# Two stacked transformer blocks on one core: the edges between ten stages done by halves of the tokens

## What is computed

```python
for l in range(2):                       # first block, 512 tokens
    f = swiglu(rmsnorm(x, g), w_gate, w_up, w_down)        # stage "F1"
    x = x + 0.5 * rmsnorm(f, post_g)
    m = token_mixing(rmsnorm(x, g), w_in, ..., w_out)      # stage "M1": three kinds of attention
    x = x + rmsnorm(m, post_g)
    f = swiglu(rmsnorm(x, g), ...)                         # stage "F1" again
    x = x + 0.5 * rmsnorm(f, post_g)
h = concatenate([meta_tokens, x])
for l in range(2):                       # second block, 528 tokens
    h = mixer_sublayer(h, ...)           # stage "M2": attention, convolutions, w_out, norm, residual
    h = ffn_sublayer(h, ...)             # stage "F2": as swiglu, with a 3-tap convolution on the hidden features
```

## Time and profile before

| | us |
|---|---|
| median of 3 runs | 3659.04 (3654.0 to 3659.16) |
| the profiled execution, its own time | 3653.45 |
| its span, first to last instruction | 3651.7 |
| PE busy | 3451.0 (95%) |
| PE weight loads busy | 2940.5 (81%) |
| DVE busy | 1738.8 (48%) |
| ACT busy | 1378.0 (38%) |
| POOL busy | 458.4 (13%) |
| mean granted TensorE clock | 0.968 of full |

### The profile page before, as it was taken

How to read it: one execution, slowest core, us unless ns; L and a number is a source line. 1 busy time by engine, 2 the same in 40 slices (tenths; PEclk the granted TensorE clock), 3 DMA queues, 4 the chain that set the end, 5 groups by cost and what they waited for, 6 DMA issues and landing times.

```text
span 3651.7 us, 54900 instructions
## 1 busy us (share of the span) xinstructions
PE 3451.0 (95%) x20422; PEld 2940.5 (81%) x20422; DVE 1738.8 (48%) x2244; ACT 1378.0 (38%) x2224; POOL 458.4 (13%) x253
## 2 busy tenths in 40 slices
PE   7999899899998999899899998988999999889998
PEld 5888666578886888666688887878999988789997
DVE  4442456444424442456444315734664266356642
ACT  3332345432224232345433323564443245534431
POOL 2000222200001000322200004202000132110000
PEclk9999999899999999899899998998999999989998
DMA  4333311123232332312133322212222221122232
GB/s 133 98 92 95 90 53 59 52 81 97 89 96 76 92 97 90 90 53 58 47 92 92 95 90 64 53 39 70 88 90 88 87 65 50 47 64 90 88 93 70
DMA packets 329965, 287.71 MB, mean 79 GB/s; under 512 B 9089, under 2 KB 325593, under 8 KB 329781
## 3 DMA queue, kind: packets, MB, share of 16 engines
q1 hardware_dynamic: 327344, 281.63, 26.0%
q10 hardware_dynamic: 2245, 3.50, 0.3%
q0 software_dynamic: 192, 0.14, 0.1%
HBM read 283.10 MB, written 5.27 MB: 79 GB/s over the span
## 4 chain that ended last, share of the span: by engine, by line
PE 87%; DVE 4%; issue 3%; ACT 3%; POOL 1%; ACTq 0%; DVEq 0%; DMA 0%; POOLq 0%
PE ps L546 24%; PE ps L547 24%; PE ps L548 24%; DVE x L676 2%; PE ps L1485 2%; PE ps L1487 1%; PE ps L1486 1%; PE ps L1070 1%; PE ps L1094 1%; PE ps L1107 1%; PE ps L578 1%; PE ps L588 1%; DVE S L670 1%; ACT xhi L616 1%; PE ps L1534 1%
## 5 line engine op out<-in xcount | busy, mean ns | idle before, releaser
L546 PE MATMUL ps<-xhi,whi 128*128 128x512 f32 (+1 forms) x3296 | 1140.6, 346 | 7.0 <-ACT r L608 5.2
L547 PE MATMUL ps<-xlo,whi 128*128 128x512 f32 (+1 forms) x3296 | 1132.4, 344 | 0.0
L548 PE MATMUL ps<-xhi,wlo 128*128 128x512 f32 (+1 forms) x3296 | 1128.8, 342 | 0.0
L529 DVE TENSOR_TENSOR wlo<-raw,whi 128x1024 fp32r<-128x1024 f32 (+1 forms) x426 | 510.8, 1199 | 1285.2 <-ACT whi L523 1282.2
L523 ACT ACTIVATE whi<-raw 128x1024 fp32r<-128x1024 f32 (+1 forms) x536 | 555.0, 1037 | 1303.4 <-PE ps L548 1243.3
L546 PEld LDWEIGHTS ps<-xhi,whi 128*128 128x128 f32 x3296 | 625.4, 190 | 99.3 <-issue 24.8
L548 PEld LDWEIGHTS ps<-xhi,wlo 128*128 128x128 f32 x3296 | 623.3, 189 | 74.6
L547 PEld LDWEIGHTS ps<-xlo,whi 128*128 128x128 f32 x3296 | 624.6, 189 | 71.8 <-issue 0.5
L548 PE MATMUL ps<-hhi,wlo 128*128 128x512 f32 (+1 forms) x1408 | 477.6, 339 | 0.0
L546 PE MATMUL ps<-hhi,whi 128*128 128x512 f32 (+1 forms) x1408 | 476.5, 338 | 0.0
L547 PE MATMUL ps<-hlo,whi 128*128 128x512 f32 (+1 forms) x1408 | 476.2, 338 | 0.0
(11 more groups left out here) (247 smaller groups left out, 3916.5 us busy)
## 6 DMA issues: line engine op xcount, KB each, us to landing
raw<-in_ffn_w_up_dram SPq DMA_DIRECT2D x176, 512.0 KB, 3.6
raw<-in_ffn_w_down_dram SPq DMA_DIRECT2D x120, 512.0 KB, 3.5
raw<-in_w_in_dram SPq DMA_DIRECT2D x94, 512.0 KB, 3.8
raw<-in_ffn_w_gate_dram SPq DMA_DIRECT2D x88, 512.0 KB, 3.8
raw<-in_w_out_dram SPq DMA_DIRECT2D x32, 512.0 KB, 3.5
raw<-in_ffn_w_down_dram SPq DMA_DIRECT2D x24, 256.0 KB, 2.8
tbias_scratch<-rev_scratch ACTq DMA_DIRECT2D x1, 3072.0 KB
y<-tbias_scratch SPq DMA_DIRECT2D x2, 1536.0 KB, 6.9
```

The costliest lines, as they stand in the source:

```text
L529: eng.tensor_tensor(wlo[slot][:, 0:n], raw[slot][:, 0:n], whi[slot][:, 0:n].bitcast(F32), ALU.subtract).then_inc(b.s.weights_split, 1)
L546: pe.matmul(o, wh, hi[:, t0:t0 + w], start=first, stop=False)
L547: pe.matmul(o, wh, lo[:, t0:t0 + w], start=False, stop=False)
L548: ins = pe.matmul(o, wl, hi[:, t0:t0 + w], start=False, stop=last)
```

## The change

Every edge is done in two halves of the tokens (256 and 256, or 264 and 264):

- Output tiles. In F stages the last pair of output chunks (m=3), in M stages the last two pairs (m=2 and 3), are made half by half (`pe_late`): first all remaining tiles for the tokens of half 0, then for half 1. Their weights must then be held all at once; they get homes in memory that is free by then (`home`: parts of the hidden tile, or of the attention's buffers).
- Norm. The squares are summed by a matmul against a full 128x128 tile of ones, in f32, which leaves the sum on all partitions (`pe_post_sum`, three matmuls; `pe_pre_sum`, one), and ACT makes the inverse root as exp(-0.5 ln(...)) for each half (`act_norm`). `pe_square_sum`, `act_rms`, `dve_inv`, `pe_spread`, `act_r` are gone.
- New x. `dve_edge` handles two chunks of one half in an instruction where it can (128 x 2 x 256): scaled y, new x, and xlo chunk by chunk. The post gain is applied when ACT copies y. The squares of new x go to y and are added by DVE (`dve_x_sum`), no longer by POOL.
- First granules. The next stage's first three granules (before: two) are split ahead, by ACT and DVE, into three `whi`/`wlo` buffers, and `pe_first` does them for half 0, then for half 1.
- The layer loops are written out, and waits outside the inner loops are on constants. The bias table of M1 is loaded later, in three DMAs. At the start x comes in two DMAs and the small loads of POOL move to SP behind them; at the end the output is stored as its quarters are ready.

The core of the diff:

```diff
+        def pe_post_sum(pe, g, h):
+            t0, w = OUT[g][h]
+            o = ps[:, sum_bank(g, "post 0") if h == 0 else sum_bank(g + 1, "post 1"), 0:w]
...
+            pe.matmul(o, ones[:, 0:P], acc[:, t0:t0 + w], start=True, stop=False)
+            pe.wait_ge(e.y_squared, 8 * (g + 1) - (1 - h) * len(LATE[g]))
+            pe.matmul(o, ones[:, 0:P], sq[0][:, t0:t0 + w], start=False, stop=False)
+            pe.matmul(o, ones[:, 0:P], sq[1][:, t0:t0 + w], start=False, stop=True).then_inc(e.norm_sums, 1)
...
+        def pe_first(pe, b, g, gb, tiles, rest=()):
...
+            for h, (t0, w) in enumerate(IN[g]):
+                pe.wait_ge(e.out_free, max(OUTS[g] - 1 + h, 0))
+                for p in range(4):
+                    now = [(n, t) for n in range(2) for t in tiles[n] if t[2] // 2 == p]
+                    pe.wait_ge(e.x_hi, 8 * g + 4 * h + p + 1)
+                    for n in range(2):
+                        if h == 0 and any(n == i and t is tiles[n][0] for i, t in now):
+                            pe.wait_ge(b.s.weights_split, gb + n + 1 + CR)
+                        for _, (bank, wcol, c, start, stop) in [i for i in now if i[0] == n]:
+                            for wt in (whi, wlo):
+                                pe.matmul(view(bank, h), wt[n][:, wcol:wcol + P], xhi[:, c, t0:t0 + w],
+                                          start=(start and wt is whi), stop=False)
+                    pe.wait_ge(e.x_lo, 8 * g + 4 * h + p + 1)
+                    for n, (bank, wcol, c, start, stop) in now:
+                        ins = pe.matmul(view(bank, h), whi[n][:, wcol:wcol + P], xlo[:, c, t0:t0 + w],
+                                        start=False, stop=stop)
+                        if h == 1 and (bank, wcol, c, start, stop) == tiles[n][-1]:
+                            ins.then_inc(b.s.granules_done, 1)
+                    if h == 0 and p == 1 and g > 0:
+                        pe_post_sum(pe, g - 1, 1)
+                if h == 0:
+                    pe.wait_ge(b.s.weights_split, gb + 2 + 1 + CR)
+                else:
+                    pe_pre_sum(pe, g, 0)
+                half = len(tiles[2]) // 2
+                for t in tiles[2][:half]:
+                    tile(h, 2, t)
+                if h == 1:
+                    pe_pre_sum(pe, g, 1)
+                for t in tiles[2][half:]:
+                    ins = tile(h, 2, t)
+            if rest:
+                pe.wait_ge(e.norm_log, pre(g, 1))
+                for t in rest:
+                    for h in range(2):
+                        ins = tile(h, 2, t)
...
+        def act_norm(act, idx, bank, dst):
+            w = dst.shape[1]
+            act.wait_ge(e.norm_sums, idx)
+            act.activation(dst, ps[:, bank, 0:w], ACT.Ln, bias=eps[:, :], scale=1.0 / D).then_inc(e.norm_log, 1)
+            act.wait_ge(e.norm_log, idx)
+            act.activation(dst, dst, ACT.Exp, scale=-0.5).then_inc(e.norm_made, 1)
...
+        def dve_edge(dve, g, ch, factor, nxt, third=None):
+            for h in range(2):
+                dve.wait_ge(e.norm_made, post(g, h))
...
+                scaled(0)
+                for p in range(4):
+                    x2 = x[:, 2 * p:2 * p + 2, c0:c0 + w]
+                    ch.wait()
+                    dve.tensor_tensor(x2, x2, t2(p), ALU.add).then_inc(e.x_new, 1)
+                    if p < 3:
+                        scaled(p + 1)
+                    if h == 0 and p == 1 and third is not None:
+                        third()
+                    if nxt is not None and p > 0:
+                        dve_x_lo(dve, g + 1, nxt, h, p - 1)
+                if nxt is not None:
+                    dve_x_lo(dve, g + 1, nxt, h, 3)
+                    dve_x_sum(dve, g + 1, h, ch)
...
+        def pe_late(pe, b, g, gb, qs, hi, lo):
...
+            for h in range(2):
+                n = 0
+                for m in LATE[g]:
...
+                    for q in range(whole, nq):
...
+                        for k in qs[q]:
+                            for o in range(2):
+                                ins = tile(h, m, q, k, o)
+                                n += 1
+                                if h == 1 and n == POST_AFTER:
+                                    pe_post_sum(pe, g, 0)
...
+            nxt = PRE[KIND_AT[g + 1]]
+            for p in range(3):
+                act_x_hi(act, g + 1, nxt, 0, p)
+            for p in range(2):
+                act_x_square(act, g + 1, 0, p)
+            act_ypart(act, b, g, gb, nq, 3, 1, col)
+            act_x_hi(act, g + 1, nxt, 0, 3)
+            act_post_norm(act, g, 1)
+            for p in (2, 3):
+                act_x_square(act, g + 1, 0, p)
+            for p in range(4):
+                act_x_hi(act, g + 1, nxt, 1, p)
+                act_x_square(act, g + 1, 1, p)
```

More of the change, by code:

```diff
@@ new lines, in act_pre_norm, with act_x_hi @@
+        def act_pre_norm(act, g, h):
+            t0, w = IN[g][h]
+            act_norm(act, pre(g, h), sum_bank(g, f"pre {h}"), r[:, t0:t0 + w])
+        def act_x_hi(act, g, col, h, p):
+            t0, w = IN[g][h]
+            c0, _ = xcols(g, h)
+            act.wait_ge(e.x_new, 8 * g + 4 * h + p + 1)
+            for c in (2 * p, 2 * p + 1):
+                ins = act.activation(xhi[:, c, t0:t0 + w], x[:, c, c0:c0 + w], ACT.Copy, scale=gain(col, LAYER[g], c))
+            ins.then_inc(e.x_hi, 1)
@@ L662, in act_yevac @@
             for o in range(2):
[L663 to L683 removed]
+                c = 2 * m + o
@@ L703, in pe_up_granule @@
                 pe.wait_ge(b.s.hidden_free, f.ev(l) + 2 * i + q // 2 + 1)
+            apart = isinstance(i, int) and not b.conv
             for o in range(2):
@@ L713, in pe_up_granule @@
-                if o == 0 and between is not None:
-                    between()
+                    bank, wcol = 4 * (q // 2) + 2 * o, kk * PAIR + o * P
+                    if apart:
+                        for h, (t0, w) in enumerate(IN[0]):
+                            ins = part_mm(pe, ps[:, bank + h, 0:w], whi[q % 2][:, wcol:wcol + P],
+                                          wlo[q % 2][:, wcol:wcol + P], xhi[:, k, t0:t0 + w], xlo[:, k, t0:t0 + w],
+                                          False, kk == 3)
+                        continue
@@ L715, in pe_up_granule, with pe_out @@
+                    ins = tile_mm(pe, b, bank, q % 2, wcol,
+                                  xhi[:, k, :], xlo[:, k, :], first and kk == 0, not first and kk == 3)
             ins.then_inc(b.s.granules_done, 1)
-        def pe_out(pe, b, l, sub, gb, qs, hi, lo, ready, second=None, order=None, begun=0):
+        def pe_out(pe, b, g, gb, qs, hi, lo, ready=None, second=None, begun=0):
             nq = len(qs)
-            def pair_of(base, m, mi):
-                pe.wait_ge(b.s.out_free, 4 * sub + base + m + 1)
+            for m in range(begun, LATE[g][0]):
+                if m == 1 and second is not None:
+                    second()
+                if m == 2:
+                    pe.wait_ge(e.out_free, OUTS[g] + 1)
@@ L774, in pe_ffn @@
+        def pe_ffn(pe, b, g, f):
+            l = LAYER[g]
+            tiles = [[(4 * (q // 2) + 2 * o, kk * PAIR + o * P, 4 * (q % 2) + kk, q % 2 + kk == 0, q == 1 and kk == 3)
+                      for kk in range(4) for o in range(2)] for q in range(3)]
+            rest = []
+            if b.conv:
+                tiles[2], rest = tiles[2][0::2], tiles[2][1::2]
+            pe_first(pe, b, g, f.gb(l), tiles, rest)
             pe_up_granule(pe, b, l, f, 0, 3)
```

874 lines of the change are left out of this document (467 added, 407 removed).

## The result

| | before | after |
|---|---|---|
| median, us | 3658.53 (4 runs) | 3537.32 (4 runs, 3533.23 to 3539.5) |
| ratio | 1 | 0.9669 (0.9657 to 0.9681) |
| span of the profiled execution, us | 3651.7 | 3534.8 |
| mean granted TensorE clock | 0.968 | 0.988 |

The kernel is 121 us faster; 159 were forecast. The spans differ by 116.9. I read first the same cuts as in the earlier trace rows: each from the end of half 0 of the late tiles to the first matmul behind the granules that are done by halves (three into M1, M2 and F2; four into F1). The first line is the start up to its second loop, the eighth the end; the three lines behind the mark are stretches between edges.

The account below looks back on a forecast made before the run. PE, 95% busy, was taken as the bound, with gains only at edges. Span 3651.7 - 144 (edges) - 13 (end) + 4 (start) - 6 (M stages) = 3492.7 us; median 3659.04 - 159 = 3500, range 3458 to 3560.

Parts of the forecast that it names:

- The edge: Nine transitions between stages: step-by-step timeline of F1 to M1; all nine to cost 76 us in place of 220, minus 144.
- The end: Kernel end, behind the last output tiles: 17 us instead of 30.3, minus 13, bounds 9 to 16.
- The start: Kernel start: later loads and four more table loads against half 0 starting early; plus 4 us, bounds -3 to +12.
- The small loads behind x: At the start: small loads queued behind 2 MB of x on SP, making DVE 0 to 7 us later.
- Inside the M stages: Four attention stages: written-out loops drop register arithmetic ahead of waits, 1.5 us a stage, minus 6, bounds 0 and 20.
- the weights cost nothing: At edges: seven granules load in about 22 us within 25; if cover fails, one or two us an edge.
- rival 2: Edges: clock falls to 1.2 GHz at new gaps, plus 8 us an edge, 3572; milder mixtures 3530 to 3570; 0.19 together.
- rival 1: Edges: half 1's waits are hidden by ACT and DVE overlap, 2 to 3 us an edge, 3445 to 3465; chance 0.14.
- rival 3: Narrow matmuls: held by weight loads of 0.190 us, 192 us more over 2628 matmuls, 3692; chance 0.03.
- The drain at a table load: Start: a skill page's 1.38 us drain per table switch, five loads 6.9 us more, start plus 11; chance 0.03.

Follow-up runs that it names:

- experiment 4: Changed kernel with squares and their sums in fp32r tiles, so the matmuls against ones run in reduced precision: 3514.69 us, ratio 0.9602.
- experiment 5: Changed kernel with one load of the table set holding both Ln and Exp ahead of the first stage: 3529.03 us, ratio 0.9643.
- experiment 6: Changed kernel with the third granule split by ACT and DVE behind half 0 of x at the start, instead of ahead: 3533.57 us, ratio 0.9654.
- experiment 2: Changed kernel with ACT's whole queue around the attention stages' late tiles reordered, third granule's low part made inside the edge: 3513.12 us, ratio 0.9602.
- experiment 1: Changed kernel with only ACT's evacuation of output pair m=1 in attention stages moved, between the sixth and seventh late granules' splits: 3541.15 us, ratio 0.9676.
- experiment 7: Changed kernel with ACT's wait for the table's store and its issue of the 3 MB copy moved behind its setup activations: 3536.76 us, ratio 0.9664.
- experiment 8: Changed kernel with three start edits: third granule behind half 0 of x, one table load, 3 MB copy behind ACT's setup: 3524.05 us, ratio 0.9628.
- experiment 10: Kernel with all winning edits and half 0's additions moved later, plus the 3 MB copy issued behind ACT's squares of first x: 3461.45 us, ratio 0.9455.

## Why the prediction was right, and where it was off

- **The edge.** The timeline that I drew up for F1 to M1 holds nearly step by step. With time 0 at 407.06: norm of half 0 at 4.2 (3.7 forecast), last xlo of half 0 at 15.1 (14.1), DVE idle from there to 17.6 (16.5), additions done at 20.0 (19.1), PE ready at 21.2 (19.6) and waiting 1.2 us at xhi of half 1 (2.0), last xlo at 28.5 (28.3), last sum at 30.8 (30.9), third granule done at 34.4 (32.7). The costs of 6.5, 7.0 and 9.3 us were measured as 6.2 to 7.4, 6.4 to 6.8, and 8.6; the 1.2 us an edge that I put on top for what no row showed was not needed.
- **One price in it was wrong.** The f32 matmul against ones: 0.24 us was read from a row that counts eight records, but each such matmul has two records, so it is 0.43. That is 8 x 0.19 = 1.5 us an edge more; experiment 4 shows that it is on the path. About half of it came back in a wait at xhi 0.8 us shorter than forecast. In the second F1 to M1 edge, where the clock stayed at 1.00, the cost is 6.4 us against the 6.1 that I had drawn up.
- **The end** came as forecast: 27.37 us less 84 matmuls (9.9) is 17.5, against 17.
- **The start** is 10.0 us later (69.57, against 48.44 and 48 wide matmuls, 11.1), inside the bounds, not 4. The tables cost 3.9 us up to there instead of 3.2, and 1.6 more by the clock behind (experiment 5). I had not seen that ACT splits the third granule ahead of all xhi (experiment 6: the first xhi matmul comes 5.5 us earlier without it). The small loads behind x, which I had feared, moved ACT's first activation from 19.80 to 21.35 only.
- **Inside the M stages** is the step that failed: "between nothing and 5 us a stage I take 1.5". No saving is to be seen; there is a loss of 6 to 12 us a stage, 35 in all, where my bounds were a gain of 0 to 20. The sentence that the weights cost nothing, with "one or two us an edge" if their cover fails, came nearest. I had counted seven granules in 22 us against 25 and found cover enough, and the loads do keep up (in experiment 2 the waits go with the same loads). What I had not asked is what else stands in ACT's queue behind a split that waits for a load: two evacuations for which PE and POOL wait. 24 us of the 35 are shown to come from that. Of the rest some 4 are a wait of 2.0 us in each M2 (up to 2170.54 in the first, for DVE's evacuation, which stands behind M2's scans); no run tested it. About 6 to 7 remain open, and so do the 8 us in the F stages, save 1.6 of slow clock in the first. That the total still fell into the range is in part luck: the edges won 13 us more than forecast, and the range was wide for other reasons.
- **The clock** (rival 2, 3530 to 3572): the time fell into its range, but for the most part it happened elsewhere. The edges run at 0.95 to 1.00, and only in three of them (the first, and both M2 to F2, behind a wait of 2.62 us) did the clock fall. It fell above all behind the new waits inside attention stages, where it adds 1.6 us or more to each.
- **The small remainder** (rival 1, 2 to 3 us an edge) did not come: no edge costs less than 6.2 us, and DVE does stand still in its middle until ACT's squares are there (2.49 us).
- **Weight loads** (rival 3): 256-token matmuls run 0.118 us apart with a load each, each load recorded at 0.19 us; the rival falls. The Trainium skill's rule (TensorE: Matmul & The Clock Gate, LDWEIGHTS), columns / 1.2 ns or 107 ns a load, is just under that pace, so nothing in this trace speaks against it; no run here shows a load's own pace.
- **The drain at a table load** (Trainium skill, ScalarE: Activation LUTs, What ACT_TABLE_LOAD costs): by it the start would be 11 us later, and it is 10. The number fits and the mechanism does not: behind each of the five loads the next activation starts 0.01 to 0.02 us later, where the page has a drain of 1.38, and experiments 5 and 6 (3.9 us and 5.5) account for the time otherwise. The measurement decides.

## What to carry to other kernels

When work is split so that PE has filler, check every in-order queue for an instruction that waits for a load and stands ahead of one that somebody waits for; in this kernel one such place, in four stages, cost 24 us where the whole change won 121. Moving the instruction that the profile names is not enough (experiment 1 won nothing); write down the whole queue by the times at which each operand is there. A wait of 3 us on PE cost nearly 5 here, since the clock was low behind it, so a few of them outweigh many small ones. And where an early step is paced by a load, making everything else earlier can move the load into another transfer's way (experiment 7).

## What the runs showed of the hardware

- After idle stretches of PE of 2.62, 2.85, 3.70 and 5.4 us in the changed kernel's trace the granted clock was at about 0.5 to 0.6 for the next 3 to 4 us. Behind shorter ones it came out both ways. In the first F1 to M1 edge it fell behind a wait of 1.20 us and one of 0.51; in the first M1 to F1 edge, behind a wait of 1.19 us in the same place, it stayed at 1.00:

```profile
431.14:434.90 3.76, 3.76 (x19) 3.76 (x20) 3.58 (x8) 2.63 (x7) 0.00 (x0) 0.55 0.02 4
728.57:732.00 3.43, 2.86 (x20) 2.46 (x20) 3.43 (x8) 2.86 (x7) 0.00 (x0) 1.00 0.00 0
```

- The same holds of one and the same wait in two executions of one program. Behind the wait of 2.46 us for a low part late in the second M2 the clock was at 1.00 in the changed kernel's profile and at 0.52 in its rerun (first line the changed kernel, second the rerun):

```profile
3087.85:3091.40 3.55, 3.55 (x29) 3.55 (x30) 0.28 (x1) 3.51 (x5) 1.13 (x1) 1.00 0.45 148
3089.16:3092.70 3.54, 3.54 (x16) 3.54 (x17) 0.26 (x1) 3.29 (x5) 1.12 (x1) 0.52 0.44 148
```

So the length of a wait alone does not tell whether the clock falls behind it. In an edge it costs 0.9 us or nothing: the first edge took 0.93 us less in the rerun, where the clock stayed at 1.00.

- An f32 matmul of 256 columns took 0.43 us from start to start, one of reduced precision 0.12.
- A 512 KB load that took 3.8 us on its own took 8.6 us (experiment 7) and 9.1 (experiment 8) while a 3 MB copy from memory to memory was under way, and 3.8 again when the copy was issued behind it (experiment 10).
